# A hybrid mixer and mixture-of-experts layer: projections that read two weight units as one moving operand

## What is computed

```python
proj = h @ w_in
q, k, v, og, a1, z, xbc, dt_raw = split_last(proj, IN_SPLITS)   # v, og, z: 512 columns each
log_a = log_sigmoid(a1 @ gla_w_a2 + gla_b_a) / GLA_TAU
o_gla = rms_norm(gla_chunk_causal(q * GLA_DK ** -0.5, k, v, log_a)) * silu(og)
xs, bm, cm = split_last(silu(causal_depthwise_conv(xbc, ...)), ...)
dt = softplus(dt_raw + ssd_dt_bias)
y = rms_norm((ssd_chunk_causal(xs, dt, a, bm, cm) + xs * ssd_d) * silu(z))
mix = concatenate([o_gla, y]) @ w_out
h = layer_norm(DEEPNORM_ALPHA * h + mix)
h = layer_norm(DEEPNORM_ALPHA * h + moe_ffn(h))   # 32 experts, three 1024x1024 matrices each
```

## Time and profile before

| | |
|---|---|
| median of 3 runs | 1058.77 us (1058.33 to 1059.17) |
| span of the profiled execution, first to last instruction | 1057.0 us |
| instructions in it | 12137 |
| TensorE matmul busy | 1021.6 us, 97% of the span |
| moved by DMA | 426.21 MB, mean 403 GB/s |

### The profile page before, as it was taken

One profiled execution on the slowest core, in us unless ns is written; L12 is line 12 of the kernel. 1 busy time (PEld: TensorE's weight loads), 2 busy tenths in 40 slices (PEclk: granted clock), 3 DMA queues, 4 the chain that ended last, 5 costly groups with the idle time before them and its releaser, 6 DMA issues.

```text
span 1057.0 us, 12137 instructions
## 1 busy us (share of the span) xinstructions
PE 1021.6 (97%) x5116; PEld 449.5 (43%) x5116; DVE 228.6 (22%) x495; ACT 143.9 (14%) x348; POOL 29.7 (3%) x50
## 2 busy tenths in 40 slices
PE   8999999999999999999999999999999999999997
PEld 7888764333333333333333333333333333333332
DVE  5453572111111111111111112211111111111112
ACT  3312331111111111011110111111111110011102
POOL 1230100000000000000000000000000000000000
PEclk9999999999999999999999999999999999999999
DMA  9894689999999999999999999999999999999995
GB/s 314 273 410 192 201 327 410 428 428 435 429 429 435 432 425 433 435 436 424 430 435 436 424 422 436 432 430 426 435 434 428 428 435 435 430 425 427 428 418 236
DMA packets 40011, 426.21 MB, mean 403 GB/s; under 512 B 6922, under 2 KB 19347, under 8 KB 23204
## 3 DMA queue, kind: packets, MB, share of 16 engines
q1 hardware_dynamic: 37940, 424.12, 95.6%
q10 hardware_dynamic: 2032, 1.53, 0.6%
HBM read 424.59 MB, written 1.05 MB: 403 GB/s over the span
## 4 chain that ended last, share of the span: by engine, by line
PE 72%; DMA 26%; ACT 1%; DVE 0%; issue 0%; SPq 0%; POOL 0%; DVEq 0%; POOLq 0%; ACTq 0%
PE bank L1200 30%; DMA ring<-in_moe_w_up 18%; PE bank L1251 15%; DMA ring<-in_moe_w_gate 8%; PE bank L1180 4%; PE bank L1172 4%; PE bank L856 3%; PE bank L871 2%; PE bank L1046 2%; PE bank L1034 1%; PE bank L988 1%; PE bank L1242 1%; PE bank L1120 1%; PE bank L949 1%; PE bank L1054 1%; PE bank L1220 1%
## 5 line engine op out<-in xcount | busy, mean ns | idle before, releaser
L1200 PE MATMUL bank<-ring,arena 128*64 128x512 f32 x1988 | 447.5, 603 | 23.8 <-DMA ring<-in_moe_w_up 20.3
L1200 PEld LDWEIGHTS bank<-ring,arena 128*64 128x64 f32 x1988 | 142.5, 139 | 298.7 <-issue 257.7
L1251 PE MATMUL bank<-ring,arena 128*64 128x512 f32 x1024 | 226.8, 595 | 1.5 <-issue 1.5
L1251 PEld LDWEIGHTS bank<-ring,arena 128*64 128x64 f32 x1024 | 71.5, 137 | 151.7 <-issue 150.2
L1641 DVE COPY arena<-bank 128x512 f32<-128x512 f32 x32 | 22.1, 692 | 326.0 <-PE bank L1251 326.0
L741 ACT ACTIVATE arena<-arena 128x512 f32<-128x512 f32 x32 | 20.1, 629 | 451.1 <-DVE arena L1628 451.1
L1180 PE MATMUL bank<-arena 64*128 64x512 f32 x256 | 72.0, 640 | 0.9 <-DVE arena L1641 0.9
L1172 PEld LDWEIGHTS bank<-arena 128*128 128x128 f32 x480 | 58.8, 196 | 22.8 <-issue 22.8
L1635 DVE TENSOR_SCALAR arena<-bank 128x512 f32<-128x512 f32 x32 | 22.1, 692 | 210.3 <-PE bank L1200 210.3
L752 ACT ACTIVATE arena<-bank 128x512 f32<-128x512 f32 x32 | 19.1, 597 | 337.4 <-PE bank L1242 337.4
L1172 PE MATMUL bank<-arena 128*128 128x128 f32 x480 | 64.5, 288 | 0.0
(11 more groups left out here) (281 smaller groups left out, 511.6 us busy)
## 6 DMA issues: line engine op xcount, KB each, us to landing
ring<-in_moe_w_down SPq DMA_DIRECT2D x25, 4096.0 KB, 29.6
ring<-in_moe_w_gate SPq DMA_DIRECT2D x24, 4096.0 KB, 25.4
ring<-in_moe_w_up SPq DMA_DIRECT2D x24, 4096.0 KB, 28.2
ring<-in_moe_w_gate SPq DMA_DIRECT2D x10, 2048.0 KB, 22.6
ring<-in_moe_w_up SPq DMA_DIRECT2D x10, 2048.0 KB, 15.2
ring<-in_moe_w_down SPq DMA_DIRECT2D x10, 2048.0 KB, 17.4
ring<-in_w_in SPq DMA_DIRECT2D x12, 1024.0 KB, 11.8
ring<-in_moe_w_gate SPq DMA_DIRECT2D x8, 1024.0 KB, 17.2
```

The source lines that it names most:

```text
L1200: ins = mm(b[h * SL:(h + 1) * SL, :], (xA[pp], xB)[q][:, k, par * SL:(par + 1) * SL], columns(unit_at(m, kt), h), start=False, stop=kt == ...
L1251: ins = mm(bank[6][h * SL:(h + 1) * SL, :], hidT[:, kt % 4, (kt // 4) * SL:(kt // 4 + 1) * SL], unit_at(2, kt)[:, h * 512:(h + 1) * 512], ...
```

## The change

`w_pair(n)` describes two neighbouring units as one operand with a unit index ahead of the k-tile. `pair_major` projects one token tile against both units at once: for each k-tile, the same stationary block of `hT`, and a moving operand of two runs of 256 columns that lie 2048 words apart, into the whole bank of 512. V, z and the output gate use it, one token tile after the other, instead of one unit after the other. V's tile 0 is done whole ahead of the `dsum_ps` matmuls; V's tile 1 is split after four k-tiles around the log gates' matmuls. The output gate's tile 0 is done whole, tile 1 is split after four k-tiles around the wait for `mix_y` and the transposes. Both units of a pair are waited for ahead of the first matmul. The transfers and the other engines' streams are as they were.

```diff
+        def w_pair(n):
+            return ring[:, n // 4, (n % 4) * HW:(n % 4 + 2) * HW].rearrange("p (u k n) -> p u k n", u=2, k=KT)
...
+            def pair_major(b, n, t, kts):
+                for kt in kts:
+                    ins = mm(b[:, :].rearrange("p (u n) -> p u n", u=2), hT[:, kt, META + t * P:META + (t + 1) * P], w_pair(n)[:, :, kt, :],
+                             start=kt == 0, stop=kt == KT - 1)
+                return ins
+            first_kts, last_kts = range(KT // 2), range(KT // 2, KT)
             pe.wait_ge(w_landed[U_V], 16)
+            pe.wait_ge(w_landed[U_V + 1], 16)
             pe.wait_ge(conv, 8)
             pe.wait_ge(cT_ok, 6)
-            token_major(bank[5][:, 0:256], U_V, 0)
+            pair_major(bank[5], U_V, 0, range(KT)).then_inc(v_ps, 1)
...
-            token_major(bank[7][:, 0:256], U_V, 1)
+            pair_major(bank[7], U_V, 1, first_kts)
             pe.wait_ge(la_ok, 1)
...
-            pe.wait_ge(w_landed[U_V + 1], 16)
-            for t, b in enumerate((bank[5], bank[7])):
-                token_major(b[:, 256:512], U_V + 1, t).then_inc(v_ps, 1)
+            pair_major(bank[7], U_V, 1, last_kts).then_inc(v_ps, 1)
...
             for hf in range(2):
-                n = U_Z + hf
-                pe.wait_ge(w_landed[n], 16)
-                for t in range(NT):
-                    for kt in range(KT):
-                        ins = mm(bank[(0, 5)[t]][:, hf * 256:(hf + 1) * 256], hT[:, kt, META + t * P:META + (t + 1) * P], wslot(n, kt),
-                                 start=kt == 0, stop=kt == KT - 1)
-                    if hf:
-                        ins.then_inc(z_ps, 1)
+                pe.wait_ge(w_landed[U_Z + hf], 16)
+            for t in range(NT):
+                pair_major(bank[(0, 5)[t]], U_Z, t, range(KT)).then_inc(z_ps, 1)
...
             for hf in range(2):
-                n = U_OG + hf
-                pe.wait_ge(w_landed[n], 16)
-                for t in range(NT):
-                    for kt in range(KT):
-                        ins = mm(bank[(6, 7)[t]][:, hf * 256:(hf + 1) * 256], hT[:, kt, META + t * P:META + (t + 1) * P], wslot(n, kt),
-                                 start=kt == 0, stop=kt == KT - 1)
-                    if hf:
-                        ins.then_inc(og_ps, 1)
-                    if hf and t == 0:
-                        pe.wait_ge(mix_y, 2)
-                        mix_transposes(bank[0], z_t, (4, 5))
-                        mix_transposes(bank[5], z_t, (6, 7))
+                pe.wait_ge(w_landed[U_OG + hf], 16)
+            pair_major(bank[6], U_OG, 0, range(KT)).then_inc(og_ps, 1)
+            pair_major(bank[7], U_OG, 1, first_kts)
+            pe.wait_ge(mix_y, 2)
+            mix_transposes(bank[0], z_t, (4, 5))
+            mix_transposes(bank[5], z_t, (6, 7))
+            pair_major(bank[7], U_OG, 1, last_kts).then_inc(og_ps, 1)
```

## The result

The changed kernel takes 1063.98 us (median of 5 runs, 1063.61 to 1064.83) against 1058.86 for the kernel before beside it (1058.33 to 1059.53): a ratio of 1.005, with a 95% interval from 1.0039 to 1.0061. That is 5.1 us slower, where 0.6 us faster was forecast.

The account below looks back on a forecast made before the run. TensorE's chain was taken to bound the first half and the transfer stream the rest; 0.07 + 0.27 + 0.28 = 0.62 us sooner, passed on one to one, gave 1058.2 us from 1058.77, range 1057.3 to 1059.3.

Parts of the forecast that it names:

- What bounds the kernel: Whole kernel: TensorE's chain from 12 to 146 us, then the expert-weight transfer stream from about 155 us to the end.
- The first link between the two: TensorE's releases before 124 us start the transfer stream; expert 1's first gate half is issued near 135.7 instead of 136.30.
- from there one to one: From the output projection to the end: the 0.62 us lead there ends the kernel 0.62 us sooner.
- five rivals: Only a small fixed part saved (0.20), whole gain (0.10), stream not sooner (0.05), operand jump costs (0.04), issued as two (0.03).
- rival 4: Joined matmuls in V, z, gate: the moving operand's jump costs time; at 40 ns each, 1061.4 us; chance 0.04.
- rival 1: V, z, gate: joins save only 1.8 ns a pair, the excess belongs to columns; q at 75.36, 1058.8 us; chance 0.20.
- The price of a join: V, z, output gate: joining saves 0.45, 0.27 and 0.28 us of TensorE time, 1.00 us in all.
- The stall ahead of q: Before the q projection: dsum_ps 3.32 us later delays v_ok; TensorE waits 0.38 us, q starts at 75.16, 0.07 sooner.
- `kdec` and `mix_y` did not stop TensorE: Meta rows and output gate's tile 1: no stall, with 0.97 us to spare for kdec and 1.31 us for mix_y.
- The sum at the output projection: Start of the output projection: 0.07 from q, 0.27 from z and 0.28 from the gate, 0.62 us sooner, near 117.3.

Follow-up runs that it names:

- f4: Changed kernel with the dsum_ps matmuls moved into the middle of V's tile 0, plus 96 padding wait instructions on TensorE; 1058.87 us against 1058.74, ratio 1.0002.
- e1: Changed kernel plus 96 instructions of already reached waits on TensorE, ahead of three of the last experts; 1059.00 us against 1058.63, ratio 1.0003.
- e4: Kernel before with only V joined and reordered, z and output gate as before; 1059.13 us against 1058.63, ratio 1.0003.
- e2: Kernel before plus 66 instructions of already reached waits ahead of three of the last experts; 1063.65 us against 1058.63, ratio 1.0047.
- f2: Kernel before plus 98 instructions of already reached waits ahead of the last experts; 1063.15 us in one run, against 1058.74.
- f3: Kernel before plus 132 waits inside the extra-tiles body that this input never runs; 1063.59 us against 1058.74, ratio 1.0048.
- f1: Kernel before plus 32 instructions of already reached waits ahead of the last experts; 1058.98 us in one run, against 1058.74.

## Why the prediction was wrong, point by point

**What bounds the kernel** was read rightly up to 1038 us: TensorE's chain in the mixer, then the stream of transfers, then the last transfer of up. The first link between the two held as well: the first gate half of expert 1 is issued at 136.35 us in after and at 136.04 in f4, against 136.30, where the output projection starts at 117.97 and 117.66, against 117.91.

```profile
136.35 10.36 SPq L412 DMA_DIRECT2D ring<-in_moe_w_gate  x2
```

**The step that failed** is "from there one to one": that what follows the edited lines repeats the kernel before, only shifted. I treated the tail as the same instructions with the same waits. They are, but the removal of 190 instructions moved the jump and its target against the blocks in which TensorE's program is brought in, and the tail has an exposed jump: it stands behind the last transfer, where every idle microsecond goes to the end. The prediction counted the instructions that go away only as matmul time, never as program length, and the profile of before shows no idle stretch there that would have warned of it. None of the five rivals has this mechanism. The only one that was slower beyond 2.1 us, rival 4 (the jump in the moving operand), had the sign and not the cause: joined records stand 429 to 430 ns apart, so the operand's jump costs nothing, as predicted. With the tail's idle stretch gone, in e1, the time of 1059.00 us lies in the predicted range, but near rival 1's 1058.8 and not 0.6 us below before.

**The price of a join** was mis-sized: 14 ns a pair for V (0.45 us / 32) and 8 to 9 for z and gate were predicted, 2.5 ns were measured. That is near rival 1's 1.8, and its q at 75.36 and its sum, 0.01 later, stand beside 75.40 and 0.06 measured; but the excess belongs neither to records, as I had it, nor to columns, as rival 1 had it. I had divided the length of a piece by its records. The records' starts show that inside a piece of 256 columns they follow one another at 215 or 216 ns in V, z and gate alike; only the first one of a piece after other work takes longer to the next start (320 ns, for z) and often the last (309 ns). In after, z has the same two: 534 and 523 ns among 429 and 430. An edge belongs to a piece and not to a record, so joining does not remove it. The chain's rows held this already: V's middle piece of 16 is 3.54 us, 0.09 above 16 times line 1054's 215.6 ns; 32 take 7.10, 0.20 above; but 64 take 14.01, again only 0.21 above. An excess that doesn't grow from 32 to 64 is no price per record. z takes 13.93 us instead of the 13.74 that I predicted. The sentence that cited the Trainium skill (TensorE: Matmul & The Clock Gate, Back-to-back issue gap) with 2.5 ns fixed for each matmul had the right size: within z, twice 215.82 less 429.14 is 2.5 ns, and z's 32 joins save 0.08 us.

**The stall ahead of q** came as worked out, and a little later. `dsum_ps` comes late, POOL's first pass starts at 62.67 (62.55 predicted, from the earlier trace rows plus 3.32), ACT's evacuation of V at 74.66 (74.54), q at 75.40 (75.16) with this wait:

```profile
75.40 7.14 PE L960 MATMUL bank<-arena,ring 128*128 128x256 f32 x32 [0.23 <-ACT arena L638]
```

TensorE was later there than predicted, as V saved less, so its wait is 0.23 us and not 0.38, and q starts 0.17 us later than before instead of 0.07 sooner. f4 shows the other side: with `dsum_ps` early, q starts at 75.13 without a wait. `kdec` and `mix_y` did not stop TensorE, as predicted.

**The sum at the output projection**: predicted 0.62 us sooner, measured 0.06 later; 0.17 lost at q against 0.08 gained in z and 0.08 in the gate, with the rest in differences of some hundredths. Whether a lead there reaches the end one to one stays open: 0.25 us, the largest lead that a kernel here had, is less than the spread of runs.

**The idle stretch's worth**: of the 4.83 us in the tail, 2.93 are the later start and 1.66 the slower matmuls behind it. Nothing hides either of them: the first output tile waits for these matmuls, and ACT's last issue of output comes 4.82 us later than in before (1058.20 after 1053.38). The 1.66 us go with the lower clock, which e4 has without an idle stretch.

## What to carry to other kernels

An edit that changes the number of an engine's instructions moves every later jump and its target; look in the profile for a jump with nothing behind it to hide an idle stretch (the tail, above all), and for an idle time that is put down to "issue" with an instruction packet beside it. This goes for both sides of a comparison, since padding made the kernel before slow (e2, f2, f3) as easily as it made the changed one fast. If a small edit gives a loss of a few microseconds far away from its lines, repeat it with some dozens of instructions of padding before its merit is judged: here this turned 1.005 into 1.0003. And read a price per instruction from pieces of different lengths, so that the edges of a piece are not taken for a part of it.

## What the runs showed of the hardware that was not expected

TensorE's program is brought in by transfers while it runs, in packets of 16384 bytes that took 0.9 to 1.4 us, 29 or 30 of them in each execution, the last ones in its final 15 us. A forward jump of some 310 instructions left TensorE idle for no time, for 1.45 us, or for 2.50 to 2.85 us, by its place alone. The kernels with an idle stretch are slower than before by 4.4 to 5.1 us, with the lower clock behind it in every trace.

One more difference between the two profiles is not the change's: from 262 to 270 us the granted clock is 0.76 to 0.81 in after and 1.00 in before, and TensorE is 1.7 us behind at 274.55 (272.87 before). But f1, whose program is that of before up to the last experts, has 0.84 and 0.73 there and the same matmuls at 274.54, and e1 has 1.00, so it differs from one execution to the next. The stream of transfers, which sets the pace later on, absorbs it, since at 1031 us the two kernels are within 0.2 us of each other.
